# A hybrid decoder layer on one core: a ring of eleven weight parts in place of ten, and the small first loads issued by ScalarE

## The reference

```python
mod = (silu(c) @ w_ada + b_ada)                 # 1024 -> 6 * 1024, one row a sequence
h = rmsnorm(x, g_pre_mix) * (1 + sc_mix) + sh_mix
proj = h @ w_in                                 # 1024 -> 3340: pooling input, q/k/v, z, a, b
mix = concat(pooling heads, gated-DeltaNet heads) @ w_out
x = x + gt_mix * rmsnorm(mix, g_post_mix)
h = rmsnorm(x, g_pre_ffn) * (1 + sc_ffn) + sh_ffn
f = moe_ffn(h)                                  # top 4 of 32 experts a token
x = x + gt_ffn * rmsnorm(f, g_post_ffn)
```

## Time and profile before

| | us |
|---|---|
| median of 3 runs | 1352.59 (1351.43 to 1357.14) |
| profiled execution | 1357.89 |
| its span | 1355.1 |
| TensorE busy | 1156.0 (85%) |
| VectorE, ScalarE, GpSimd busy | 265.9, 241.3, 251.7 |
| mean granted TensorE clock | 0.93 |

### The profile page before, as it was taken

How to read it: one execution, slowest core, us unless ns; L and a number is a source line. 1 busy time by engine, 2 the same in 40 slices (tenths; PEclk the granted TensorE clock), 3 DMA queues, 4 the chain that set the end, 5 groups by cost and what they waited for, 6 DMA issues and landing times.

```text
span 1355.1 us, 30215 instructions
## 1 busy us (share of the span) xinstructions
PE 1156.0 (85%) x12197; PEld 619.1 (46%) x12198; DVE 265.9 (20%) x709; ACT 241.3 (18%) x560; POOL 251.7 (19%) x495
## 2 busy tenths in 40 slices
PE   3899999998777997998699997986568976699994
PEld 3778869845432443443244443432223432244442
DVE  1044527464310110111011111110001110011113
ACT  2241322232110111111011111110001110011112
POOL 4030103011121221222122222121112211122220
PEclk9898999996799998999899999997889988899997
DMA  9835843254599999999999099999999999999895
GB/s 314 305 127 187 309 122 140 71 217 167 175 379 428 428 408 395 428 427 427 426 428 428 21 399 428 426 427 427 429 427 426 429 428 427 427 426 416 358 417 202
DMA packets 69393, 463.07 MB, mean 342 GB/s; under 512 B 5703, under 2 KB 23352, under 8 KB 44673
## 3 DMA queue, kind: packets, MB, share of 16 engines
q1 hardware_dynamic: 68152, 460.43, 83.1%
q0 software_dynamic: 800, 0.91, 0.2%
q10 hardware_dynamic: 355, 0.42, 0.1%
HBM read 455.27 MB, written 6.55 MB: 341 GB/s over the span
## 4 chain that ended last, share of the span: by engine, by line
PE 61%; DMA 30%; issue 3%; SPq 3%; DVE 2%; ACT 1%; DVEq 0%; ACTq 0%
PE psum L599 20%; DMA weights<-in_w_down 17%; PE psum L626 10%; DMA weights<-in_w_gu 9%; PE psum L898 5%; PE psum L559 3%; PE psum L577 3%; DMA weights<-in_w_ada 2%; PE psum L609 2%; PE psum L1142 2%; PE psum L903 2%; PE psum L853 1%; DMA out<-weights 1%; PE psum L510 1%; PE psum L523 1%
## 5 line engine op out<-in xcount | busy, mean ns | idle before, releaser
L599 PE MATMUL psum<-weights,work 128*32 128x512 f32 x3392 | 415.0, 639 | 120.7 <-DMA weights<-in_w_gu 73.2
L599 PEld LDWEIGHTS psum<-weights,work 128*32 128x32 f32 x3392 | 110.8, 115 | 394.2 <-issue 280.6
L2295 POOL TENSOR_SCALAR level_masks_sb<-work 128x128 f32<-128x128 f32 x159 | 123.9, 789 | 662.1 <-PE psum L617 662.1
L626 PE MATMUL psum<-weights,work 128*32 128x256 f32 x3392 | 197.1, 381 | 16.4 <-DMA weights<-in_w_down 16.0
L2139 DVE TENSOR_TENSOR work<-psum,work 128x256 f32<-128x256 f32 x53 | 22.5, 425 | 863.4 <-PE psum L609 863.4
L626 PEld LDWEIGHTS psum<-weights,work 128*32 128x32 f32 x3392 | 104.2, 110 | 93.0 <-DMA weights<-in_w_down 23.6
L1600 ACT COPY work<-psum 128x512 f32<-128x512 f32 x53 | 31.0, 586 | 512.1 <-PE psum L599 512.1
L559 PE MATMUL psum<-work 128*32 128x256 f32 x1296 | 83.5, 392 | 0.0
L898 PE MATMUL psum<-work,weights 128*128 128x288 f32 x320 | 81.0, 410 | 0.0
L559 PEld LDWEIGHTS psum<-work 128*32 128x32 f32 x1296 | 44.5, 115 | 56.1 <-issue 39.1
L898 PEld LDWEIGHTS psum<-work,weights 128*128 128x128 f32 x320 | 60.0, 190 | 17.4 <-issue 1.8
(11 more groups left out here) (362 smaller groups left out, 987.0 us busy)
## 6 DMA issues: line engine op xcount, KB each, us to landing
weights<-in_w_gu SPq DMA_DIRECT2D x128, 2048.0 KB, 30.1
weights<-in_w_down SPq DMA_DIRECT2D x64, 2048.0 KB, 23.0
weights<-in_w_ada SPq DMA_DIRECT2D x12, 2048.0 KB, 13.2
weights<-in_w_in SPq DMA_DIRECT2D x6, 2048.0 KB, 13.0
weights<-in_w_out SPq DMA_DIRECT2D x1, 4096.0 KB, 13.2
weights<-in_state_ssm SPq DMA_DIRECT2D x8, 384.0 KB, 5.6
out<-weights SPq DMA_DIRECT2D x1, 3072.0 KB, 16.9
weights<-in_w_in SPq DMA_DIRECT2D x1, 1072.0 KB, 12.1
```

What stands on the lines that cost most here:

```text
L599: last = mm(bank(GB)[SLOTS * n:SLOTS * n + SLOTS, :], xTm[:, k % 2, k // 2, :], gu[:, k % 2, 512 * n:512 * n + 512], start=k == 0, stop=k ...
L626: last = mm(bank(TB)[SLOTS * q:SLOTS * q + SLOTS, 0:QW], hT4[:, k % 4, k // 4, :], dn[:, k % 4, QW * q:QW * q + QW], start=k == 0, stop=k ...
L2295: ins = g.tensor_scalar(selG[:, c, :], iota_bd if c == 2 else iota, cur[:, 0, c:c + 1], cur[:, 1, c:c + 1], ALU.is_equal, ALU.mult)
```

## The change

Two things in one edit. The ring gets an eleventh slot, number 10. It lies in the tensor `work`, which grows by FRONT = 3840 words a partition in front, and takes the first 256 words of `x_sb` as well, so its first load stands behind the store of the prompt's x1. PERIOD becomes 11 (for a loop body must hold a whole number of ring turns: 66 parts), so TensorE's program is two passes over 11 experts and 10 experts written out behind. The loads ahead of the expert stage are eleven, shifted by one against the points at which slots come free. The final tiles move to slots 0 to 2. The 24 small loads leave GpSimd for ScalarE, between the `hT` copies and the first unit's read. Two semaphores become one to make room, and the scratch for GpSimd's DMA descriptors is cut.

```diff
--- before.py
+++ after.py
@@ -47,10 +47,10 @@
 RING = 4
 
 
-NSLOT, SLOT_W = 10, 4096
-PLACES = (4, 5, 6, 7, 1, 2, 0, 3, 8, 9)
+NSLOT, SLOT_W = 11, 4096
+PLACES = (4, 5, 6, 7, 10, 1, 2, 0, 3, 8, 9)
 PER_EXPERT = 6
-PERIOD = 5
+PERIOD = 11
 SEQS = 1 + NSEQ
 
 
@@ -172,11 +172,11 @@
 
 SEMS = """acc_add bguT c_in c_silu ch_act ch_dve ch_pool const_in conv_done cum cur_set dexp diff_ps egates
  fin_in fin_y gT g_ready ga gate_done gate_ps gated gates gex gm_in gu_a w_in0 w_in1 w_in2 w_in3 w_in4
- w_in5 w_in6 w_in7 w_in8 w_in9 gu_ps gu_read d_read h2 h2T h2T_v h2_ps hT_a hT_s hid hid_ps hid_step hist_in kdec kk_ps kqm
+ w_in5 w_in6 w_in7 w_in8 w_in9 w_in10 gu_ps gu_read d_read h2 h2T h2T_v h2_ps hT_a hT_s hid hid_ps hid_step hist_in kdec kk_ps kqm
  ks_ps kq_ps vm_ps lg_sb sp_new seq_in rb_in kvT_ps kv_tok lmat mix_ps ml modG modG_st modT modT_ps mod_sb norm_ps oT oT_ps o_ms o_ps
  o_root p1 p1_ps poolT pool_ps pooled proj_ps qk_ps qkd qkdT qkdT_ps qs_sb rank_done ring0 ring1
  ring2 ring3 root router_ps rr rt_in s_new s_ps s_silu s_taps sc_ps total_ps sel sel_step selg setup_ps setup_sb
- rk2 rk_root tt_done un_ps sgT sgT_ps sig silu_done slot_used small_in softplus_a softplus_v sp_e sq ssm_in ssm_out ssq stats_set t0
+ rk2 tt_done un_ps sgT sgT_ps sig silu_done slot_used small_in softplus_a softplus_v sp_e sq ssm_in ssm_out ssq stats_set t0
  u_ready tailT_ps tail_rows tail_st tap3 tn_ps top_e tu_done u0 u0_ps u_sb vec_in vmask vn vn_ps wout_in wpool_in x1
  x1_st x2T_ps xT_ps xTm xTm_ps x_in xg xg_ps xn xn2 y_ps y_sb y_st z_sb """.split()
 
@@ -195,14 +195,16 @@
         s = {n: ctx.enter_context(nc.semaphore(n)) for n in SEMS}
 
 
-        Wt = sb("weights", [P, NSLOT * SLOT_W])
+        Wt = sb("weights", [P, (NSLOT - 1) * SLOT_W])
         WM = 11664
-        Mt = sb("work", [P, WM])
+        FRONT = 3840
+        Mt = sb("work", [P, FRONT + WM])
         lmask_t = sb("level_masks_sb", [P, LEVEL_COLS // 2])
         lmask = lmask_t[:, :].bitcast(BF16)
         ps_t = ctx.enter_context(nc.psum_tensor("psum", [P, 8, 512], F32))
         G0, G1, DD = Arena(Wt, 16384), Arena(Wt, 16384, 16384), Arena(Wt, 8192, 32768)
-        W, M = Arena(Wt, NSLOT * SLOT_W), Arena(Mt, WM)
+        W, M = Arena(Wt, (NSLOT - 1) * SLOT_W), Arena(Mt, WM, FRONT)
+        last_slot = Arena(Mt, SLOT_W)
 
         def bank(b, n=1):
             return ps_t[:, b:b + n, :].rearrange("p b n -> p (b n)")
@@ -219,11 +221,11 @@
         QKT = [G1.at(14400 + 768 * c, H, P) for c in range(2)]
         Us, QKTs = G1.at(15936, H, NS), G1.at(15936 + 192, H, NS)
         Sp = Lm[0]
-        FB = 6 * SLOT_W
+        FB = 0
         fin_x = W.at(FB, 3, D)
         fin_g = [W.at(FB + 3072, D), W.at(FB + 3072, D), W.at(FB + 4096, D)]
         fin_junk = W.at(FB + 5120, D)
-        fin_t = [W.at(FB + 6144, D), W.at(FB + 7168, D), W.at(SLOT_W, D)]
+        fin_t = [W.at(FB + 6144 + D * c, D) for c in range(3)]
         X0 = Arena(Wt, SLOT_W)
         xt = [X0.at(D * c, D) for c in range(3)]
         mixjunk = X0.at(3 * D, D)
@@ -543,10 +545,10 @@
             return PLACES[s_no % NSLOT], s_no // NSLOT
 
         def slot_gu(n):
-            return W.at(SLOT_W * n, 2, 2 * FF)
+            return last_slot.at(0, 2, 2 * FF) if n == NSLOT - 1 else W.at(SLOT_W * n, 2, 2 * FF)
 
         def slot_d(n):
-            return W.at(SLOT_W * n, 4, D)
+            return last_slot.at(0, 4, D) if n == NSLOT - 1 else W.at(SLOT_W * n, 4, D)
 
         def experts_pe(pe, mm, tr):
             XB, SB, GB, TB = 0, 1, 2, 3
@@ -747,24 +749,25 @@
             sp.wait_ge(s["xn2"], 2)
             sp.wait_ge(s["ssq"], 7)
             sp.dma_start(iota_bd, cc("iota_bd")).then_inc(s["seq_in"], 16)
+            load(0, 4)
             sp.wait_ge(s["mix_ps"], 4)
-            load(0, 4)
             load(0, 5)
+            load(1, 0)
             sp.dma_start(bgu_rows, b_gu[0].rearrange("e (n c) -> (e n) c", n=4)).then_inc(s["rb_in"], 16)
             for q in range(NQ):
                 sp.dma_start(b_down_sb[NE * q:NE * q + NE, :], b_down[0][:, QW * q:QW * q + QW]).then_inc(s["rb_in"], 16)
             store_x1(2)
             sp.wait_ge(s["x2T_ps"], 5)
             sp.wait_ge(s["ssq"], 9)
-            load(1, 0)
+            load(1, 1)
             sp.wait_ge(s["vm_ps"], 2 * H)
             sp.wait_ge(s["vmask"], H // 2)
-            load(1, 1)
+            load(1, 2)
             sp.wait_ge(s["s_new"], 2 * H)
             sp.dma_start(ssm_sample[0].rearrange("b h k v -> k b h v"), Ssm).then_inc(s["ssm_out"], 16)
             sp.wait_ge(s["ssm_out"], 32)
-            load(1, 2)
             load(1, 3)
+            load(1, 4)
             sp.wait_ge(s["x1_st"], 48)
 
             sp.wait_ge(s["cum"], 2)
@@ -1334,6 +1337,26 @@
                 fn(hT[:, k, 0:SEQ], bank(4 + k // 2)[:, 256 * (k % 2):256 * (k % 2) + 256], ACT.Identity,
                    scale=modT[:, 1, k, 0:1], bias=modT[:, 0, k, 0:1]).then_inc(s["hT_a"], 1)
 
+
+            act.wait_ge(s["ch_pool"], 1)
+            for i in range(4):
+                r = 64 * (i % 2)
+                act.dma_start(wpbd[r:r + 64, i // 2, r:r + 64], w_pool[0, i]).then_inc(s["wpool_in"], 16)
+            act.dma_start(alog, a_log.to_broadcast([P, H])).then_inc(s["small_in"], 16)
+            act.dma_start(dtb, dt_bias.to_broadcast([P, H])).then_inc(s["small_in"], 16)
+            act.dma_start(gdnw, gdn_norm_w.to_broadcast([P, DH])).then_inc(s["small_in"], 16)
+            ba = b_ada.rearrange("a (u j n) -> a u j n", j=4, n=P)
+            for j in range(4):
+                rows = slice(32 * j, 32 * j + 32)
+                for i in range(2):
+                    u = 4 + 6 * i
+                    act.dma_start(b_row[rows, 2 * i:2 * i + 2, :], ba[:, u:u + 2, j].to_broadcast([32, 2, P])
+                                  ).then_inc(s["small_in"], 16)
+                    gp = (g_post_mix, g_post_ffn)[i].rearrange("a (u j n) -> a u j n", j=4, n=P)
+                    act.dma_start(gpost[rows, 2 * i:2 * i + 2, :], gp[:, :, j].to_broadcast([32, 2, P])
+                                  ).then_inc(s["small_in"], 16)
+            act.dma_start(lmask_t[:, :], cc("levels")).then_inc(s["small_in"], 16)
+
             def silu_tile(h):
                 act.wait_ge(s["conv_done"], CONV_ORDER.index(h) + 1)
                 fn(qkvT[:, h, 0:SEQ], qkvT[:, h, 0:SEQ], ACT.Silu).then_inc(s["silu_done"], 1)
@@ -1441,7 +1464,7 @@
                            ).then_inc(s["poolT"], 1)
                 if u == 15:
                     act.wait_ge(s["rk2"], 1)
-                    fn(r2, r2, ACT.Sqrt).then_inc(s["rk_root"], 1)
+                    fn(r2, r2, ACT.Sqrt).then_inc(s["rk2"], 1)
                 if u == 16:
                     tokens(0, PA)
                     tokens(1, PB)
@@ -1815,7 +1838,7 @@
 
             def value_scales():
 
-                v.wait_ge(s["rk_root"], 1)
+                v.wait_ge(s["rk2"], 2)
                 own(tt(beta, beta, r2, ALU.mult))
 
             def residual_scales():
@@ -2177,26 +2200,6 @@
             for i in range(2):
                 own(g.memset(sq_s[i], 0.0))
 
-
-            for i in range(4):
-                r = 64 * (i % 2)
-                g.dma_start(wpbd[r:r + 64, i // 2, r:r + 64], w_pool[0, i]).then_inc(s["wpool_in"], 16)
-            g.dma_start(alog, a_log.to_broadcast([P, H])).then_inc(s["small_in"], 16)
-            g.dma_start(dtb, dt_bias.to_broadcast([P, H])).then_inc(s["small_in"], 16)
-            g.dma_start(gdnw, gdn_norm_w.to_broadcast([P, DH])).then_inc(s["small_in"], 16)
-            ba = b_ada.rearrange("a (u j n) -> a u j n", j=4, n=P)
-            for j in range(4):
-                rows = slice(32 * j, 32 * j + 32)
-                for i in range(2):
-                    u = 4 + 6 * i
-                    g.dma_start(b_row[rows, 2 * i:2 * i + 2, :], ba[:, u:u + 2, j].to_broadcast([32, 2, P])
-                                  ).then_inc(s["small_in"], 16)
-                    gp = (g_post_mix, g_post_ffn)[i].rearrange("a (u j n) -> a u j n", j=4, n=P)
-                    g.dma_start(gpost[rows, 2 * i:2 * i + 2, :], gp[:, :, j].to_broadcast([32, 2, P])
-                                  ).then_inc(s["small_in"], 16)
-            g.dma_start(lmask_t[:, :], cc("levels")).then_inc(s["small_in"], 16)
-
-
             g.wait_ge(s["u_sb"], 2)
             g.wait_ge(s["setup_sb"], 4)
             g.wait_ge(s["const_in"], 16 * N_CONST)
@@ -2331,7 +2334,7 @@
     import concourse.bacc as bacc
     from concourse.bass_utils import run_bass_kernel_spmd
 
-    nc = bacc.Bacc("TRN2", target_bir_lowering=False, num_devices=1)
+    nc = bacc.Bacc("TRN2", target_bir_lowering=False, num_devices=1, dynamic_dma_scratch_size=1024)
     arrays = program(nc, inputs)
     r = run_bass_kernel_spmd(nc, [arrays], core_ids=[0])
     return tuple(r.results[0][f"out_{i}"] for i in range(len(_OUTS)))
```

## The result

The changed kernel takes 1335.03 us, the median of four runs (1334.27 to 1337.83), against 1352.69 for the kernel before: a ratio of 0.9867, with an interval of 0.984 to 0.9894. That is -17.7 us where I had forecast -7.0. The profiled executions differ by more, 1357.9 to 1334.3, mostly because the one of before was 5.2 us above its median.

A forecast was written before the change was run, and what follows sets the result against it. The expert stage was taken as bound by the weight stream, except where TensorE's rounds hold it up. +1.9 - 4.9 - 3.5 + 9.4 - 4.9 - 5.0 = -7.0 us on 1352.6 gave 1345.6, range 1336 to 1355.

The forecast's parts named there:

- terms 1, 2, 4 and 5: Eleventh slot's gains, in order: -4.9 us at part 17, -3.5 first dry spell, -4.9 after second spell, -5.0 at the end.
- e12: Expert 12 by turn, counted from 0; its first slot release, ending the second dry spell, now lets in part 83.
- Term 2: An earlier slot release lets in part 35 instead of 34, so the stream's first dry spell vanishes: -3.5 us.
- Rival E: The first dry spell only moves and final loads still crawl, end gaining 1.0: +0.5 us, 1353.1; chance 0.13.
- term 3: TensorE's one remaining loop jump, straight after part 65, lies on the path: 6.4 wait plus 3.0 clock, +9.4 us.
- Rival D: Jumps back inside one expert miss the fetch too, four times 9.4 in e12: +30.6 us, 1383; chance 0.03.
- The four turns removed, costed at nothing: TensorE's former five loop jumps lie where the weight stream is the bound, so removing them gives nothing.
- e31: The last expert by turn, counted from 0, in the stretch where TensorE is the bound and its rounds were forecast unchanged.
- my -8.9: Expert-stage sum without the small loads: -4.9 - 3.5 + 9.4 - 4.9 - 5.0 us.
- term 6: Front: small loads moved to ScalarE gain 3.0 us but delay TensorE's fourth unit; net +1.9, bounds -1.3 and +15.6.
- Rival C: ScalarE's load issues block on full queues, from about 0.67 us each: front +15.6, total +6.7 us, 1359.3; chance 0.08.
- term 5: At the end, last part and queued final loads land earlier, so the final stage starts at TensorE's end: -5.0 us.

The follow-up runs named there:

- the best version: Changed kernel with PERIOD 22 and the 24 small loads on GpSimd, held behind ScalarE's first hT copy: 1323.36 us, ratio 0.9797.
- ten slots without turns: Kernel before, ring of ten, with PERIOD 20 in place of 5, so no jump between experts: 1348.14 us, ratio 0.9976.
- GpSimd late: Kernel before, GpSimd keeping the 24 small loads but starting them only at ScalarE's first hT copy: 1347.35 us, ratio 0.9959.
- loads alone: Kernel before with only the 24 small loads moved from GpSimd to ScalarE, behind the hT copies: 1350.87 us, ratio 0.9983.
- loads early: Changed kernel with ScalarE's 24 load issues moved ahead of the hT copies, behind its first square root: 1338.78 us, ratio 0.9896.
- after again: The changed kernel, unedited, measured a second time on the same chip as three other runs: 1335.65 us, ratio 0.9884.
- turn taken out: Changed kernel with PERIOD 22 in place of 11, so TensorE's code never jumps back between experts: 1328.33 us, ratio 0.9815.
- the ring alone: Changed kernel with the 24 small loads back on GpSimd, keeping the eleven slots and the loop of eleven experts: 1336.93 us, ratio 0.9889.
- the two traces with 35.5: Traces of the loads alone (1350.87 us) and the kernel without turns, in which the fourth ada part lands at 35.5 us.

## Why the prediction was wrong in size and right in mechanism

**The slot, terms 1, 2, 4 and 5: right, one of them short.** The traces show -4.9 at part 17, -3.3 more at part 34, -4.9 between e12's release and part 83, and -5.9 from part 161 to the first final step (forecast -5.0). Of the last, 1.2 us are the shorter gaps below, which leaves -4.7.

Term 2, the first dry spell, was put at -3.5, and 1.4 us more appear between parts 34 and 65. The landings say where: from part 35 to part 40 the ten-slot kernels take 25.5 to 26.0 us and the eleven-slot ones 24.4 to 24.7, and from part 40 to part 65 all take 123.7 to 123.9. So the spell had cost 4.7 us: I had counted the empty columns, and not that the parts just behind them land late too. Why they do isn't shown.

By ratios alone, the best version over the two without its slot (ten slots without turns, GpSimd late) is 0.9797 / (0.9976 x 0.9959) = 0.9861, or -18.8 us, with an interval of about 5 us to either side from the three. I had -18.3. Rival E, in which the first dry spell only moves and the end gains 1.0, is false on both counts, though the final issues still crawl a little.

**A check by the traces.** Whole times differ by 10 us, but the stretch from the issue of the state store to ScalarE's first final step is nearly the same in all traces of one ring. In us:

```
ten slots, five turns (before, loads alone, GpSimd late)        980.8  981.1  979.4
ten slots, no turn                                              978.8
eleven slots, one turn (after, ring, loads early, after again)  967.5  967.8  965.9  966.4
eleven slots, no turn (turn taken out, best of both)            958.7  958.1
```

By the means the slot gives -20.4, the five turns of before and their gaps cost 1.7, and the one turn left costs 8.5: -13.6 together.

**The turn, term 3: on the path, taken 1 us too dear.** Forecast +9.4. The difference between part 65's landing (-19.2) and e12's release (-11.0) is +8.2, the check above gives 8.5, and the times 7.0 and 9.3. The wait was even longer than in the earlier trace rows, 7.46 against 6.97, but the clock fell less: the 64 matmuls lost 1.4 us instead of 3.0. That half of the term I had read from one row at another place, as if the clock's answer to a wait were fixed.
The Trainium skill (Runtime: NRT & Kernel Launch, Instruction fetch mechanics) says that a taken branch outside the window held stalls for a fetch. The trace agrees in so far as the one jump between bodies waits (7.46 us, and 0.37 without it). Rival D, in which the jumps inside an expert miss as well, is false: one wait of that size is in the whole trace.

**The four turns removed, costed at nothing: the step that failed in the ring's sum.** "Taking them out gives nothing" was read from where the turns lie: where the stream is the bound, their waits should be hidden. Two things are against it.
First, between parts 83 and 161 the stream itself takes 387.1 to 387.3 us in the three kernels with five turns, and 385.9 to 386.2 in all others, the one with ten slots and no turn among them (386.0). About 1.2 us (1.1 in the table) were not hidden.
Second, looped code also has longer gaps between all experts, 0.58 us against 0.38, and these are on the path where TensorE is the bound. The changed kernel writes its last ten experts out; from the round behind part 161 to e31's it gains 1.2 us (1181.7 to 1318.0 before, 1164.6 to 1299.8 after).
Together that is -2.3 in the trace, and ten slots without any turn measured -3.2 us [-5.5, -0.8].

So the ring's account, from my -8.9: -1.2 for the first dry spell, -1.2 for the turn, -2.3 for turns and gaps removed, +0.3 for the end. That makes -13.3, which is what the traces show behind the state store; the time of the ring alone was -15.0 [-19.3, -10.7].

**The small loads, term 6: the second step that failed.** Forecast +1.9, measured -2.3 [-5.0, +0.4]. Three of its parts were wrong.
First, the gain: I took the queue's own share of DMA time, 3.3 us, as all that it costs the ada parts. The fourth lands 6.4 us earlier in the changed kernel (39.4 to 33.0), as with GpSimd's loads late (33.1), though only 3.9 us earlier in the two traces with 35.5, where the weights' queue moved nearly as much (13.40 and 13.25 MB in 40 us); the cause of that difference isn't shown. The rates show why the loads cost more than their share. These are the DMA rates of the first 40 us, in 1 us columns, with the queues (packets, MB, share of 16 engines), first of the changed kernel:

```profile
GB/s 0 115 157 189 330 382 334 219 312 363 387 387 387 389 381 391 385 387 389 381 389 387 397 377 387 385 391 389 383 387 373 380 357 373 381 383 389 389 385 385
...
q1 hardware_dynamic: 6827, 13.49, 94.6%
```

and of the ring alone, with the loads on GpSimd's queue:

```profile
GB/s 0 105 141 198 317 398 358 204 277 323 344 179 328 367 389 383 381 332 299 350 381 383 387 391 385 311 340 315 324 317 366 382 385 387 382 377 368 372 365 388
...
q1 hardware_dynamic: 5887, 11.62, 85.5%
q0 software_dynamic: 800, 0.91, 9.0%
```

While the small loads flow (here in bursts at 6 to 13, 17 to 20 and 24 to 31 us), all queues together move mostly 300 to 340 GB/s instead of 387. The weights' queue q1 moves 1.87 MB less in the 40 us, twice the 0.91 MB of the loads themselves; at 387 GB/s that is 4.8 us, and I had taken 3.0.
The Trainium skill (DMA: Bandwidth & Descriptors, Issuing engines are not separate DMA queues) says that another issuer saves only sequencer time. The experiment agrees: issued early by ScalarE, the loads delay the fourth ada part too, to 37.5. What helped was mostly that the change also moves them in time.
Second, the issues took 0.55 us each (13.2 in all), not 0.38. Rival C needed 0.67 and had priced them at 0.95; it is false, but the bounds were needed. One issue of the 24 took 1.40.
Third, I had the issues begin behind the hT copies. They run beside them, from 36.31, which gave back 3.7 us. The stall of TensorE (3.80 us) and its cost in clock (17.35 - 15.79 = 1.6 us, forecast 1.5) came as forecast; in the two traces with 35.5 the cost was 2.7 to 2.8 us.
The net is not settled better than its interval. With ScalarE's loads the state store is issued at 350.6, 352.3, 361.4 and 361.4 in four traces, with GpSimd's early ones at 351.3, 352.1 and 360.2: means of 356.4 and 354.5, a difference near my +1.9, but lost in the spread. The medians of the loads alone say -2.3. Which of the three parts carries the 4.2 us between the two stays open.

**The number.** The misses point the same way: -4.4 in the ring and -4.2 for the loads, on top of -7.0. The sum, -15.6, is beside the second measurement (-15.7) and 2.4 short of the first (-18.0). That it comes so close is partly luck, since the loads' term has an interval of 2.7 us to either side. Terms 1, 3 and 4 were inside the bounds that I gave, and term 5 is once the gaps are taken off. The first dry spell gave more than the one price I had for it, the turns removed had no bounds, and the loads' -2.3 is below my -1.3, though its interval reaches above it. My range was built from rivals, each with one term off; it did not allow for several terms off in the same direction.

## What to carry to other kernels

A slot more in a ring is worth one part at each point where the stream waits for its user, and it can be counted from the trace. A turn of the loop costs nearly its whole wait and the clock behind it where that engine is the bound (8 us here), and a little elsewhere too, and looped code has longer gaps wherever that engine leads; give what you write off as hidden a bound as well. Small loads beside a stream that something waits for cost 1.6 (by ScalarE) to 2.1 times (by GpSimd) their own bytes here; move them behind it in time, and leave them on an idle engine, since the issues hold up the engine that makes them (3.8 us of TensorE's time here).

## What the runs showed of the hardware that I had not expected

Executions of one kernel differ by up to 11 us, and much of it can be read in the records: from 40 to 350 us the time at half clock (1.2 GHz of 2.4) was 50.6 us in the profile of before and 40.3 in that of the changed kernel, though TensorE's work there is the same. An example is sixteen matmuls at 312.55 in before (L1142), with the same sixteen in the changed kernel at 304.79 (L1145) below them:

```profile
312.55 9.00 PE L1142 MATMUL psum<-weights,work 128*128 128x512 f32 x16
```
```profile
304.79 7.13 PE L1145 MATMUL psum<-weights,work 128*128 128x512 f32 x16
```

So of the 9.6 us between the two state stores about half, by an estimate of (50.6 - 40.3) / 2 = 5 us, is that execution's clock and not the change; it is about what the spans (23.0 us apart) have over the medians (17.7). More than half may be the execution's own: ten slots without turns, whose front is that of before line by line, has 41.0 us at half clock and its state store at 352.1, 8.1 us earlier.

ScalarE issues DMAs while its activations run (36.28 and 36.31 above), mostly at 0.45 us each and up to 0.62, with one of 1.40, where seven at the start took 0.41 on average.
